# A two-layer decoder trunk: dilated tokens kept in natural order and read with a stride

## The reference

```python
DILATED_GROUPS = ((128, 1), (512, 4), (2048, 16))
BLOCK = 128

def to_phase_blocks(x, dil):
    B, S = x.shape[:2]
    rest = x.shape[2:]
    L = S // dil
    x = jnp.swapaxes(x.reshape((B, L, dil) + rest), 1, 2)
    ...

def dilated_group_attention(q, k_cat, v_cat, dil, w_phase):
    qb = to_phase_blocks(q, dil)
    s = jnp.einsum("bpnihd,bpnjhd->bpnhij", qb, k_cat)
    s = jnp.where(valid[None, None, :, None], s, -jnp.inf)
    lse = jax.nn.logsumexp(s, axis=-1)
    p = jnp.exp(s - lse[..., None])
    o = jnp.einsum("bpnhij,bpnjhd->bpnihd", p.astype(v_cat.dtype), v_cat)
```

## Time and profile before

| | us |
|---|---|
| median of 3 runs | 1804.24 (1803.23 to 1804.55) |
| the profiled execution | 1803.23 |
| its span | 1801.4 |
| PE busy | 1513.2 (84%) |
| DVE busy | 1184.3 (66%) |
| ACT busy | 702.2 (39%) |
| POOL busy | 511.1 (28%) |

### The profile page before, as it was taken

How to read it: one execution, slowest core, us unless ns; L and a number is a source line. 1 busy time by engine, 2 the same in 40 slices (tenths; PEclk the granted TensorE clock), 3 DMA queues, 4 the chain that set the end, 5 groups by cost and what they waited for, 6 DMA issues and landing times. The chain is left out here.

```text
span 1801.4 us, 19305 instructions
## 1 busy us (share of the span) xinstructions
PE 1513.2 (84%) x6688; PEld 1125.1 (62%) x6688; DVE 1184.3 (66%) x1442; ACT 702.2 (39%) x762; POOL 511.1 (28%) x430
## 2 busy tenths in 40 slices
PE   6867139489999996599999999999989489999991
PEld 3323017366677763488888888888877366667760
DVE  3999982666557663777576775776862666567653
ACT  3333342344555461432432323324232244555441
POOL 2677610023222221343141340422400123222220
PEclk9987559579999998699999999999999589999996
DMA  3430100338888973421121221212212738888854
GB/s 155 193 140 0 47 0 1 140 110 336 352 360 357 373 324 142 178 82 59 58 82 46 70 70 47 82 50 78 68 37 82 323 123 360 344 369 351 367 213 163
DMA packets 44846, 303.08 MB, mean 168 GB/s; under 512 B 9488, under 2 KB 10256, under 8 KB 30992
## 3 DMA queue, kind: packets, MB, share of 16 engines
q1 hardware_dynamic: 34304, 284.98, 40.0%
q0 software_dynamic: 9648, 16.80, 2.6%
q10 hardware_dynamic: 864, 0.94, 0.1%
HBM read 295.34 MB, written 25.69 MB: 178 GB/s over the span
## 5 line engine op out<-in xcount | busy, mean ns | idle before, releaser
L630 POOL TENSOR_TENSOR KQ<-rope_ab 64x512 f32<-64x512 f32 x96 | 173.3, 1805 | 391.1 <-DVE rope_ab L1226 387.5
L1135 DVE TENSOR_TENSOR wgl<-WR,wgh 128x2048 fp32r<-128x2048 f32 x66 | 148.3, 2288 | 174.3 <-ACT wgh L744 171.4
L1409 PE MATMUL PS<-WR,SC 128*128 128x512 f32 x528 | 233.2, 594 | 3.4 <-ACT SC L778 1.6
L810 ACT ACTIVATE wh<-wraw 128x1024 fp32r<-128x1024 f32 x80 | 84.4, 1058 | 275.3 <-PE PS L1469 252.5
L1409 PEld LDWEIGHTS PS<-WR,SC 128*128 128x128 f32 x528 | 98.8, 190 | 117.4 <-issue 115.4
L931 DVE SCALAR_TENSOR_TENSOR SC<-SC 128x512 f32<-128x512 f32 x144 | 153.2, 1136 | 0.0
L1311 PE MATMUL PS<-HT,WR 128*128 128x512 f32 x256 | 121.8, 639 | 36.1 <-DVE SC L920 34.0
L1135 DVE TENSOR_TENSOR wul<-WR,wuh 128x2048 fp32r<-128x2048 f32 x66 | 148.0, 2284 | 0.7 <-ACT wuh L744 0.7
L744 ACT ACTIVATE wgh<-WR 128x2048 fp32r<-128x2048 f32 x66 | 122.4, 1904 | 61.9 <-DMA WR<-w_gate 61.9
L744 ACT ACTIVATE wuh<-WR 128x2048 fp32r<-128x2048 f32 x66 | 122.7, 1906 | 30.4 <-PE PS L1383 19.5
L1226 DVE TENSOR_TENSOR rope_ab<-PS,rope_sb 32x512 f32<-32x512 f32 x192 | 131.9, 687 | 2.6
(11 more groups left out here) (246 smaller groups left out, 3242.1 us busy)
## 6 DMA issues: line engine op xcount, KB each, us to landing
WR<-w_gate SPq DMA_DIRECT2D x33, 2048.0 KB, 12.2
WR<-w_up SPq DMA_DIRECT2D x33, 2048.0 KB, 16.6
WR<-w_down SPq DMA_DIRECT2D x33, 2048.0 KB, 14.0
wraw<-w_qkv SPq DMA_DIRECT2D x72, 512.0 KB, 3.3
WR<-w_in SPq DMA_DIRECT2D x8, 1024.0 KB, 4.8
WO<-w_out SPq DMA_DIRECT2D x1, 4096.0 KB, 14.7
xn_dram<-HTQ SPq DMA_DIRECT2D x8, 512.0 KB, 2.7
HT<-y_dram SPq DMA_DIRECT2D x8, 512.0 KB, 6.2
```

What stands on the lines that cost most here:

```text
L630: nc.gpsimd.tensor_tensor(to, cos, sin, ALU.add).then_inc(rope_done, 1)
L1135: V.tensor_tensor(lo[:, kts, :], raw[:, kts, :], hi[:, kts, :].bitcast(F32), ALU.subtract).then_inc(done, 1)
L1409: ins = M.matmul(PS[3 + h][:, :], hidT[:, ft, :], wd[b][:, ft, h * 512:(h + 1) * 512], start=ft == 0, stop=ft == FT - 1)
```

## The change

The keys and queries of the groups 1 and 2 stay in the order of the tokens in `KQ`. POOL adds without a permutation. The two DVE instructions of the row of maxima (one for group 0, one for the groups 1 and 2) become one over all three groups, which reads its inputs contiguously. In `scores` and `scores_t` PE reads the tiles of the groups 1 and 2 with `slice(n, T, NT)`, as stationary and as moving operand. The ACT copy (L823 to L830) stays as it is and copies the tokens in the order in which they are.

```diff
@@ POOL, attention loop
                     for h in range(2):
                         rows = slice(h * HEAD, (h + 1) * HEAD)
-                        to, cos, sin = dst[h][0:HEAD, g, :], rope_ab[rows, 2 * (t % 2), :], rope_ab[rows, 2 * (t % 2) + 1, :]
-                        if g > 0:
-                            to = to.rearrange("p (n t) -> p t n", n=NT)
-                            cos, sin = (ap.rearrange("p (t n) -> p t n", n=NT) for ap in (cos, sin))
-                        nc.gpsimd.tensor_tensor(to, cos, sin, ALU.add).then_inc(rope_done, 1)
+                        ins = nc.gpsimd.tensor_tensor(dst[h][0:HEAD, g, :], rope_ab[rows, 2 * (t % 2), :], rope_ab[rows, 2 * (t % 2) + 1, :], ALU.add)
+                        ins.then_inc(rope_done, 1)
@@ DVE, maxima_row(h)
-                    one = "p (o t n) -> p o n t"
-                    V.tensor_tensor(Qh[h][HEAD:HEAD + 1, 0, :], PS[1][0:1, :], rowt[0:1, :], ALU.min)
-                    V.tensor_tensor(Qh[h][HEAD:HEAD + 1, 1:, :].rearrange("p g (n t) -> p g n t", n=NT),
-                                    PS[1][0:1, :].rearrange(one, o=1, n=NT).to_broadcast([1, NG - 1, NT, P]),
-                                    rowt[0:1, :].rearrange(one, o=1, n=NT).to_broadcast([1, NG - 1, NT, P]), ALU.min).then_inc(row_done, 1)
+                    one = "p (o t) -> p o t"
+                    V.tensor_tensor(Qh[h][HEAD:HEAD + 1, :, :], PS[1][0:1, :].rearrange(one, o=1).to_broadcast([1, NG, T]),
+                                    rowt[0:1, :].rearrange(one, o=1).to_broadcast([1, NG, T]), ALU.min).then_inc(row_done, 1)
@@ PE, scores(h)
-                            keys = slice((n + 1) * P - w, (n + 1) * P)
-                            ins = M.matmul(PS[4 + s][:, at:at + w], q[:, g, packed(n)], k[:, g, keys],
+                            keys = slice((n + 1) * P - w, (n + 1) * P) if g == 0 else tile_of(g, n)
+                            ins = M.matmul(PS[4 + s][:, at:at + w], q[:, g, tile_of(g, n)], k[:, g, keys],
@@ PE, scores_t(h)
-                            queries = slice(n * P, n * P + w)
-                            ins = M.matmul(PS[4 + s][:, at:at + w], k[:, g, packed(n)], q[:, g, queries],
+                            queries = slice(n * P, n * P + w) if g == 0 else tile_of(g, n)
+                            ins = M.matmul(PS[4 + s][:, at:at + w], k[:, g, tile_of(g, n)], q[:, g, queries],
```

More of the change, by code:

```diff
@@ L1445, in _ @@
             with pe.Fori(0, NP_HEADS) as i:
-                def packed(n):
-                    return slice(n * P, (n + 1) * P)
                 def tile_of(g, n):
```

## The result

The changed kernel took 1848.85 us (median of 4 runs, 1848.21 to 1849.09) where the kernel before took 1803.9 in the same measurement. The ratio is 1.0249, 95% interval 1.0231 to 1.0267: 45 us slower. The forecast was 1808.8 us with a range up to 1832; the sign was right, the size wrong by a factor of ten, and the time lies outside the range.

The account below looks back on a forecast made before the run. The prediction took PE in the attention loop as the bound and summed 0 (POOL) + 0 (DVE) + 4.6 us (PE) onto 1804.24 to get 1808.8 us. The range was 1804.0 to 1832, the forecast's own 1807 to 1811.

Parts of the forecast that it names:

- What bounds the kernel: Attention loop of 594 us: PE is the bound, busy for 72.21 of 73.60 us in one pair of heads.
- POOL's add, 0: POOL's adds for groups 1 and 2: dropping the permutation gives 0, at most 0.1 us.
- The row of maxima, 0: DVE, each pair: one contiguous instruction saves 9 to 13 us of DVE, but PE does not wait, so 0.
- the slack of head 1: Before scores_t(1): the row of maxima of head 1 was there 1.29 us before PE came to it.
- PE reads with a stride, 384 instructions at 12 ns: scores and scores_t, groups 1 and 2: each strided instruction costs 12 ns more, 4.6 us in the loop.
- The upper bound, 70 ns: Strided instructions of scores and scores_t: at most 210 - 140 = 70 ns more each, 26.9 us.
- Rival (b): scores and scores_t: all 384 strided instructions pay about 70 ns, 1831 us; only the 256 fp32 ones, 1822; chance 0.23.
- 150 or more apart, the moving side pays: Sign in scores_t: matmul starts 150 ns or more apart would mean the strided moving operand pays.
- Rival (c): scores and scores_t: both strided operands from one buffer hinder each other, 23 to 30 ns each, 1813 to 1816; chance 0.12.
- (a): scores and scores_t: strided loads cost 0 to 3 ns each, up to 1.2 us, 1805 us; chance 0.22.
- (d): scores_t(1): PE held by head 1's row of maxima, now 0.83 us earlier; 6.6 us faster, 1797.6; chance 0.03.

Follow-up runs that it names:

- the doubled row: Kernel before, with DVE doing the strided minimum of the row of maxima twice in each row; ratio 1.0043, 7.8 us slower.
- the probe: Kernel before, with 15 groups of 12 matmuls or transposes added after PE's last one; fp32 starts 112 ns apart contiguous, 233 with the stationary operand at 16 bytes.
- the 8-byte kernel: Queries and keys of groups 1 and 2 stored with a phase's tokens 8 bytes apart, both operands strided; ratio 1.0022 against the kernel before.

## Why the prediction was wrong

**What bounds the kernel** was right: PE, in the loop, and 43.3 of the 45 us are PE's.

**POOL's add, 0:** right. The adds still take 1.8 us, and the hole is still 1.4 us.

**The row of maxima, 0:** right. It takes 1.75 us, the upper bound being 2.04; the doubled row showed that the slack of head 1 is what was read.

**PE reads with a stride, 384 instructions at 12 ns:** the count was right, the price wrong. In scores_t it is 233 - 111 = 122 ns, 256 x 122 = 31.2 us; in scores 0.38 us a bank, 12.2 us; 43.4 in all. The step that failed is the transfer from the transposes: "the 120 ns have the same load and almost the same length (210) that the new ones should have". They do not have the same load. In the same rows, the contiguous load of a transpose lasted 140 ns and the contiguous load of the scores 191; the stride brought them to 212 and 329. The spacing hid this. Contiguous transposes stood 109 ns apart in the probe, strided ones 121, so a load that became 70 ns longer moved the start of the next by 12: the load had time in hand. What held the contiguous ones is most likely their moving side: 256 contiguous fp32 columns stood 216 ns apart in scores_t of the kernel before, and half of that is 108 (an estimate; no run took it apart). The scores had nothing in hand, as the prediction itself found ("it is the weight load that sets it"); its 103 ns for L1518 were a little too low, since the starts there stood 109 to 114 ns apart, but that changes nothing in the argument. The difference of 51 ns between two contiguous loads of 128 columns was in the rows and was passed over; it was the sign that the two loads are not the same work. Why the load of a transpose is shorter stays open.

**The upper bound, 70 ns,** failed for the same reason: it was the increase of the shorter load, and so the range ended at 1832. A bound in proportion would have held. A load record of the scores is 191 - 111 = 80 ns longer than the pace that it sets. Without these 80 the load of a transpose grows from 60 to 130 ns, 2.2 times, and 2.2 x 111 = 241: 130 ns more. This is an estimate made afterwards from the earlier trace rows.

**Rival (b)** named the mechanism, that every one of the 384 pays because the scores' loads are read in another way or the moving side pays; both are so, but its price, 70 ns, was too low as well, at 1831 us. Its argument against itself, that the moving side keeps up in the rounded L1518, holds for the rounded operand and not for fp32. The sign "150 or more apart, the moving side pays" was no sign of that: with the stationary operand alone strided the starts are as far apart (1.98 us a bank against 2.06). **Rival (c)** fell: both strided cost hardly more than one. **Rivals (a) and (d)** fell.

The Trainium skill's rule on lines of 16 bytes, in "SBUF — State Buffer" (Door 1: The DMA port swizzle) and "Advanced Engine Details and Errata" (SBUF Cachelines), was nearer than the rows that were set against it: at 16 bytes both operands pay, at 8 bytes in fp32 almost nothing. It does not hold to the letter. Two hits to a line are to be enough by it, but two bf16 elements to a line (8 bytes) cost 0.88 ns a column against 0.42 contiguous (216 ns for 512). And the first of the two sections counts a stride of up to 4 fp32 as free, which is the stride that cost 45 us here. The 32-byte transposes, 113 ns apart where those at 16 bytes stood 120, were the exception: ordinary loads at 32 bytes stood 240 apart.

## What to carry to other kernels

An operand for TensorE whose elements lie 16 bytes apart costs twice and more what neighbours cost, on either side, once that side sets the pace; let the engine that writes the operand put it in order, if it can do so for nothing, as POOL did here (3.71 us against 3.70) and ACT did not (1.06 against 0.60). Before a price is carried from one instruction to another, compare the two where neither is burdened: here the load of the same 128 contiguous columns lasted 140 ns in one and 191 in the other. A difference in spacing tells the price only where the thing that changed also set the pace before; else it is what was left after the slack.

## What the runs showed of the hardware that was not expected

- fp32 and bf16 moving operands cost about 1.8 ns for each 16 bytes walked over, whatever the number of elements in them, no less than the contiguous pace, and no more beyond 16 bytes (bf16 0.45, 0.67, 0.88, 1.33, 1.77, 1.80 ns a column at 4 to 32 bytes). Ordinary loads cost 1.82 at 16 bytes and 1.88 at 32; at 8 bytes they cost almost nothing extra (the 8-byte kernel), and at 12 they were not measured at the full clock. Rounded moving operands and transposes stay at 0.86 to 0.94 at 16 and 32 bytes.
- These times do not follow TensorE's clock: loads at 16 bytes stood 233 ns apart at a granted clock of 1.00 and of 0.50, and 512 bf16 moving columns at 16 bytes 900 ns at both.
- POOL's add of 64x512 took 2.33 us beside DVE's subtraction of two SBUF tiles and about 1.3 without it; one wait on DVE gave 9 us.
